# Sending half the rows of one weight transfer in eight pieces of eight rows

## The reference, cut to what matters

```python
def expert_block(args):
    x_blk, e = args
    return (jax.nn.silu(x_blk @ w_gate[e]) * (x_blk @ w_up[e])) @ w_down[e]
```

## Time and profile before

| | us |
|---|---|
| median of 3 runs | 1035.82 (1033.69 to 1036.24) |
| the profiled execution | 1037.0 |
| its span, first to last instruction | 1035.2 |
| PE busy in the span | 978.1 (94%) |
| DVE busy, ACT busy | 436.1 (42%), 182.2 (18%) |
| read from HBM | 300.47 MB |

### The profile page before, as it was taken

How to read it: one execution, slowest core, us unless ns; L and a number is a source line. 1 busy time by engine, 2 the same in 40 slices (tenths; PEclk the granted TensorE clock), 3 DMA queues, 4 the chain that set the end, 5 groups by cost and what they waited for, 6 DMA issues and landing times.

```text
span 1035.2 us, 15494 instructions
## 1 busy us (share of the span) xinstructions
PE 978.1 (94%) x6439; PEld 545.9 (53%) x6439; DVE 436.1 (42%) x811; ACT 182.2 (18%) x419; POOL 28.5 (3%) x88
## 2 busy tenths in 40 slices
PE   7999998999999999999999999989889988898996
PEld 6788875576666665568764533333233323332332
DVE  2868377173655566402232753622213222222213
ACT  2233334210000001214342101100001011001111
POOL 8100000000000000000000000000000000000000
PEclk9999999999999999999999999999999999999999
DMA  8424022484776689552142799999999999999994
GB/s 353 171 95 158 3 82 83 180 359 189 285 286 283 283 344 423 216 217 89 75 163 82 297 417 428 428 424 428 427 424 430 426 427 428 426 429 425 417 414 177
DMA packets 29377, 302.49 MB, mean 292 GB/s; under 512 B 5888, under 2 KB 6016, under 8 KB 10752
## 3 DMA queue, kind: packets, MB, share of 16 engines
q1 hardware_dynamic: 29312, 301.53, 71.1%
HBM read 300.47 MB, written 1.05 MB: 291 GB/s over the span
## 4 chain that ended last, share of the span: by engine, by line
PE 68%; DMA 21%; SPq 6%; DVE 2%; ACT 1%; issue 1%; DVEq 0%; ACTq 0%
DMA slot<-in_moe_w_up_dram 11%; PE PS L1635 11%; PE PS L1239 10%; PE PS L1234 9%; PE PS L1684 8%; PE PS L1978 6%; SPq L666 6%; PE PS L1997 5%; DMA AR<-in_moe_w_up_dram 4%; DMA XH<-in_moe_w_up_dram 4%; PE PS L1957 2%; PE PS L1464 2%; PE PS L1582 2%; DMA slot<-in_moe_w_down_dram 2%; PE PS L1932 1%; PE PS L1678 1%
## 5 line engine op out<-in xcount | busy, mean ns | idle before, releaser
L1635 PE MATMUL PS<-XH,slot 128*128 128x256 f32 x512 | 113.3, 379 | 1.7 <-DVE XH L2502 0.9
L1635 PEld LDWEIGHTS PS<-XH,slot 128*128 128x128 f32 x512 | 97.1, 190 | 21.3 <-issue 8.9
L1234 PE MATMUL PS<-XH,slot 128*128 128x256 f32 x432 | 97.6, 383 | 0.0
L1234 PEld LDWEIGHTS PS<-XH,slot 128*128 128x128 f32 x432 | 80.7, 190 | 12.4 <-issue 1.2
L1997 PE MATMUL PS<-slot,ATT 128*32 128x512 f32 x576 | 68.9, 629 | 13.7 <-DMA slot<-in_moe_w_up_dram 13.7
L1978 PE MATMUL PS<-slot,ATT 128*32 128x512 f32 x544 | 65.8, 607 | 6.5 <-issue 3.6
L1239 PE MATMUL PS<-slot,XH 128*128 128x256 f32 (+4 forms) x224 | 71.7, 476 | 0.0
L1978 PE MATMUL PS<-slot,MASKS 128*32 128x512 f32 x576 | 64.3, 594 | 2.0 <-DMA slot<-in_moe_w_down_dram 1.5
L2551 DVE SCALAR_TENSOR_TENSOR AR<-AR 128x384 f32<-128x384 f32 (+1 forms) x112 | 59.9, 612 | 0.0
L1957 PE MATMUL PS<-AR,DIAG 128*128 128x512 f32 x120 | 57.6, 605 | 0.0
L1239 PEld LDWEIGHTS PS<-slot,XH 128*128 128x128 f32 x224 | 42.0, 190 | 26.1 <-issue 14.8
(11 more groups left out here) (467 smaller groups left out, 1197.4 us busy)
## 6 DMA issues: line engine op xcount, KB each, us to landing
slot<-in_moe_w_gate_dram SPq DMA_DIRECT2D x18, 2048.0 KB, 35.9
slot<-in_moe_w_up_dram SPq DMA_DIRECT2D x18, 2048.0 KB, 33.9
slot<-in_w_ffn_dram SPq DMA_DIRECT2D x16, 2048.0 KB, 8.4
slot<-in_moe_w_down_dram SPq DMA_DIRECT2D x16, 2048.0 KB, 36.8
AR<-in_ada_w_dram SPq DMA_DIRECT2D x16, 1536.0 KB, 14.4
AR<-in_moe_w_gate_dram SPq DMA_DIRECT2D x9, 2048.0 KB, 35.2
AR<-in_moe_w_up_dram SPq DMA_DIRECT2D x8, 2048.0 KB, 34.3
AR<-in_moe_w_down_dram SPq DMA_DIRECT2D x7, 2048.0 KB, 36.5
```

Source lines behind the costliest of these rows:

```text
L1234: ins = pe.matmul(dst, w[:, c * width + col:c * width + col + n], HT[:, c, :], start=(c == 0), stop=(c == KC - 1))
L1635: ins = pe.matmul(PS[:, b, (f % 2) * T:(f % 2 + 1) * T], slots[s][:, c * 512 + f * P:c * 512 + (f + 1) * P], HT[:, c, :], start=(c == 0), ...
```

## The change

The first part of the gate matrix of the last pair's first expert, `(NM - 1, 0, 0, 0)`, is no longer one transfer of 128 rows. It is one transfer of rows 0 to 63 and eight transfers of 8 rows each for rows 64 to 127, in that order, in the place where the one transfer stood. The second expert's transfer of the same part follows as before. All of them add 16 to the same semaphore, so `project_part` waits for 16 x (1 + 9) = 160 in place of 32. No other transfer and no computation is changed.

```diff
         PARTS = {(NM - 2, 1): 2, (NM - 2, 2): 2, (NM - 1, 0): 2, (NM - 1, 1): 4, (NM - 1, 2): 4}
...
+        SPLIT_PART = (NM - 1, 0, 0, 0)
+        ROW_SPLITS = [(0, P // 2)] + [(r, r + 8) for r in range(P // 2, P, 8)]
...
                         if (m, kind) == (NM - 2, 1):
                             part = lambda v: v.rearrange("p (h n) -> p h n", h=2)[:, :, f * w // 2:(f + 1) * w // 2]
-                        sp.dma_start(part(RING[u % NR]), part(matrix(kind, experts[k]))).then_inc(part_loaded[m, kind][f], 16)
+                        to, fro = part(RING[u % NR]), part(matrix(kind, experts[k]))
+                        for r0, r1 in ROW_SPLITS if (m, kind, f, k) == SPLIT_PART else ((0, P),):
+                            sp.dma_start(to[r0:r1], fro[r0:r1]).then_inc(part_loaded[m, kind][f], 16)
...
             def project_part(m, kind, f):
-                pe.wait_ge(part_loaded[m, kind][f], 32)
+                pe.wait_ge(part_loaded[m, kind][f], 16 * (1 + len(ROW_SPLITS) if (m, kind, f) == SPLIT_PART[0:3] else 2))
```

## The result

The changed kernel takes 1043.93 us (median of 3 runs, 1043.84 to 1044.1) where the one before takes 1035.82: the ratio is 1.0078, interval 1.0058 to 1.0097, 8.1 us slower. The forecast was 1034.6. The profiled execution has a span of 1042.2 us, 7.0 more than before.

What follows compares the result with a forecast made beforehand. The prediction took DMA weight loading, ended by the later-finishing eight engines, as the bound. Moving bytes off them gave -1.25 us, with issue cost zero and toll 0.3 us absorbed: 1035.82 - 1.25 = 1034.6 us, range 1033.1 to 1037.6.

Steps and rivals of the forecast that it cites:

- What bounds the kernel: To the end: DMA engines move weights without pause, and the last transfer, landing at 1023.15 us, sets the end.
- Bytes per engine: At the split part: eight engines carry 32 KB more, eight 32 KB less, shifting each group by 1.25 us.
- The toll of a small transfer: In the DMA queue: each small piece costs extra, 0.3 us for eight, or 16.8 us at the far end.
- near end: Low bound of the small-transfer toll: 0.04 us each, read from 84 KB of columns behind a 512 KB transfer.
- Rival D: At the split part: each small transfer holds its engines 2.1 us unoverlapped; +8.4 us, 1044.3 us; chance 0.05.
- If the small pieces ride the early eight: At the kernel's tail: the engines finishing last end 1.25 us sooner, and so does the kernel; chance 0.55.
- The level at one half: At the load's end: DMA share near 0.50 for three microseconds, eight engines dry; predicted to shrink.
- late eight: At the load's end: the eight engines that carry on 3 to 7 us after the other eight run dry.
- the cap of 1.48: At the last down projection: PE's waits for down weights total 1.48 us, the most this tail can give.
- The issue on SP: On SP at the split part: eight more issues take 3.5 us, absorbed by waits on the full queue; cost zero.
- The rule on halves: At the split part: cited skill rule that transfers to disjoint halves only queue on the same engines; no term given.
- instruction fetch on those eight: From 590 to 1024 us: 26 instruction-fetch packets on eight engines delay each by 3.5 us; argued.

Runs made afterwards that it cites:

- eight small pieces on own rows: Against the kernel before, only rows 0 to 63 of the part sent, in eight transfers of every fourth row of a 32-row block, rows 64 to 127 omitted: 1034.69 us.
- the free runs: Against the kernel before, the part sent as even and odd rows (0.9999), or as four transfers of every fourth row (0.9992).

## Why the prediction was wrong

**What bounds the kernel** held. The last transfer sets the end, and the whole 7.01 us of its delay came out in the span.

***Bytes per engine*** is the step that failed. It counted bytes rightly and turned 32 KB into 1.25 us by the 26.1 GB/s per engine of the kernel before. That rate was read where every engine writes its own rows. For the pieces of the change it does not hold: a row took 0.672 us for 0.317. And it took its own time on each engine to be the only effect, where all 16 engines were slowed together (no packet of the 123 under 0.507 us). The bounds of that step, 0 and 1.25 us either way, came from the same rate and could not hold the result.

***The toll of a small transfer*** was right at its near end as far as number goes: nine column pieces cost 0.9 us (none to 2.3), and eight small pieces on own rows show no dip. What it left out is what a piece does to the transfers around it. The columns of the earlier trace rows, from which I took the toll, stand in a nearly empty queue and can't show that. Of the Trainium skill's rule that is cited there, the words are "under 64 KB"; the pieces, of 64 KB, stand at its edge.

**Rival D** gave 1044.3 and 1043.93 was measured, but by another way. It had each small transfer hold its engines for 2.1 us. Two halves with no small piece cost 5.3 us, and eight small pieces on own rows nothing. The agreement of the number is chance, and the run that followed the change with spread pieces (1044.46) would have been read as a proof of D if it had stood alone.

***If the small pieces ride the early eight***: the tail was read rightly as far as the runs show. The level at one half vanished in the changed kernel, and taking bytes from the late eight shortened it from three windows to one and gave 2.0 us by the ratio (-0.3 to -3.5), 1.0 by the medians, around the cap of 1.48. But the gain of 1.25 us could not be had this way: small pieces that move load from the late eight must write rows of the late eight, and those are the ones that clash.

***The issue on SP*** cost nothing, as said: twelve issues took 5.93 us, four took 4.48. The eight up issues behind them took 24.76 us for 19.20 because the queue drained slowly, not because of the extra issues: they took 24.49 in the run of the two halves, which has one issue more and not eight.

**The rule on halves.** The Trainium skill (DMA: Bandwidth & Descriptors, Rules for kernel authors) says that transfers to disjoint halves only queue up on the same engines. The prediction cited that and gave it no term in the sum; measured, two halves lose 5.3 us to one whole.

**What stays open**: why the engines that are on their own rows slow down as well, and why the rate in a dip is about half whether 64, 16 or 8 rows lie together. The PE wait of 4.58 us for a transfer issued ahead of the pieces shows that they do; no view shows where the packets wait. The Trainium skill (DMA: Bandwidth & Descriptors, Back-pressure in remote DMA) tells, for transfers between cores, of a full SBUF port that holds up other engines on the same path; no run here tells whether that is it. That the engine of a row goes by its place in the transfer (so that even rows, and every fourth row, come out with their owners) is argued from the free runs, since no view numbers the engines. And no run tests what makes eight engines late; the prediction's cause, instruction fetch on those eight, stays argued.

No version was faster than the kernel before by sending all its bytes; four transfers of every fourth row (0.9992, 0.9978 to 1.0006) are its equal.

## What to carry to other kernels

While the queue is the bound, split a transfer by columns, or by rows with a stride that still spans all 128 (strides 2 and 4 were tried here), and not into blocks of rows: 1 MB in two halves of 64 rows cost 5.3 us, in even and odd rows nothing. A price per engine worked out as bytes by rate holds only for the row pattern at which the rate was read; before using it for another, ask which rows each engine will write. And in a DMA-bound stretch read the GB/s beside the share: here the share stayed at 1.03 while the rate halved.

## What the runs showed of the hardware that was not expected

A few transfers to ill-placed rows slow all 16 engines to 222 GB/s, from 418, transfers issued earlier included (a part issued at 970.05, before the pieces, made PE wait 4.58 us). The same nine transfer sizes cost 3.5, 7.7 or 8.1 us by which rows they hold. The effect is tied to the rows in SBUF and not to those in HBM (+5.8 and -0.1 us). And one megabyte in halves shows two dips and costs 5.3 us, four show one dip and cost 12.9: it looks as if early and late engines pass the pieces at different times, so that one megabyte is paid for twice (argued).
